# A two-layer attention encoder: second attention's outputs in 512-query groups, last norm on token rows, and query low halves one step behind

## The reference

```python
# layer 0: differential attention, 8 heads, two components of 64
s = einsum('bqhcd,bkhcd->bhcqk', q, k) * scale + rel_bias     # then masked softmax p
a = p[:, :, 0] - lam * p[:, :, 1]
o = rms_norm(einsum('bhqk,bkhe->bqhe', a, v), subln_w) * (1 - lam_init)
# layer 1: latent attention, 16 heads, 64 + 32 (rotary) query and key columns, 64 value columns
p = softmax(masked((q_nope @ k_nope + q_rope @ k_rope) * scale))
o = einsum('bhqk,bkhe->bqhe', p, v)
# each layer then: o @ w_o, norm, square(relu(u @ w1)) @ w2, norm
```

## Time and profile before

| | |
|---|---|
| Median of 3 runs (least, most) | 2934.26 us (2934.16, 2934.52) |
| Profiled execution | 2934.04 us |
| Its span, instructions | 2932.4 us, 37871 |
| Busy: TensorE, VectorE, ScalarE, GpSimd | 91%, 56%, 40%, 11% |
| First attention, a head of 427.50 to 490.40 | 62.90 us |
| Second attention, two heads from 1705.27 | 31.63 and 31.83 us |

### The profile page before, as it was taken

The page is one execution under the profiler, slowest core; times in us unless marked ns, Lnnn a source line. Parts: engine busy times, 40 slices in busy tenths (PEclk is TensorE's granted clock), DMA queues, the critical chain, the costliest instruction groups (busy, mean ns, idle before and its releaser), DMA issues.

```text
span 2932.4 us, 37871 instructions
## 1 busy us (share of the span) xinstructions
PE 2668.8 (91%) x12716; PEld 2189.5 (75%) x12716; DVE 1654.3 (56%) x2830; ACT 1163.9 (40%) x2093; POOL 328.5 (11%) x346
## 2 busy tenths in 40 slices
PE   3899989879999999999997888888699999999996
PEld 2677777767788888887776777777577888888884
DVE  4477777747653443543757777777376233232356
ACT  2365666634512213123454665566245122130323
POOL 0000000001110000160324222222010000000000
PEclk8999999989999999999999999999899999999997
DMA  8233333363342331412331111111633111111122
GB/s 316 74 90 103 111 93 104 92 224 90 101 136 85 90 118 50 137 57 68 117 95 23 28 29 30 29 27 43 220 90 87 57 50 50 43 50 50 50 80 79
DMA packets 333440, 254.17 MB, mean 87 GB/s; under 512 B 41192, under 2 KB 303639, under 8 KB 332319
## 3 DMA queue, kind: packets, MB, share of 16 engines
q1 hardware_dynamic: 317518, 194.21, 22.9%
q0 software_dynamic: 14736, 50.34, 5.6%
q10 hardware_dynamic: 1088, 8.39, 0.7%
HBM read 215.12 MB, written 33.59 MB: 85 GB/s over the span
## 4 chain that ended last, share of the span: by engine, by line
PE 63%; DVE 13%; ACT 11%; issue 9%; DMA 3%; DVEq 0%; ACTq 0%; SPq 0%; POOL 0%
PE PA L1693 31%; PE SC L1693 26%; DVE H L1219 2%; DVE soft L1608 2%; ACT H L749 2%; DVE W L1128 1%; ACT X L1054 1%; ACT X L765 1%; PE TB L1700 1%; DMA x_rows<-in_x 1%; ACT W L702 1%; PE SC L1801 1%; PE VB L1785 1%; DVE X L1630 1%; DMA attention_out<-ostage 1%
## 5 line engine op out<-in xcount | busy, mean ns | idle before, releaser
L1693 PE MATMUL PA<-U,W 128*128 128x512 f32 x3840 | 950.3, 402 | 81.5 <-DVE W L1128 44.4
L1693 PEld LDWEIGHTS PA<-U,W 128*128 128x128 f32 x3840 | 726.0, 191 | 251.9 <-issue 57.2
L702 ACT ACTIVATE W<-raw 128x1024 fp32r<-128x1024 f32 (+2 forms) x262 | 260.1, 994 | 816.4 <-PE PA L1693 390.1
L1693 PE MATMUL SC<-U,W 128*128 128x512 f32 x2064 | 481.1, 391 | 4.0 <-DVE W L1128 3.7
L1693 PEld LDWEIGHTS SC<-U,W 128*128 128x128 f32 x2064 | 387.2, 188 | 90.2 <-DVE W L1128 4.9
L1128 DVE TENSOR_TENSOR W<-raw,W 128x1024 fp32r<-128x1024 f32 (+2 forms) x262 | 315.4, 1204 | 99.6 <-ACT W L702 98.3
L1693 PE MATMUL PA<-H,W 128*128 128x512 f32 x1536 | 358.6, 392 | 3.2 <-DVE W L1128 3.2
L1693 PE MATMUL SC<-H,W 128*128 128x512 f32 x1536 | 354.4, 390 | 0.0
L1693 PEld LDWEIGHTS PA<-H,W 128*128 128x128 f32 x1536 | 288.5, 189 | 64.3 <-DVE W L1128 3.6
L1693 PEld LDWEIGHTS SC<-H,W 128*128 128x128 f32 x1536 | 288.4, 188 | 60.7 <-issue 1.0
L1392 DVE SCALAR_TENSOR_TENSOR X<-PA,aff,X 128x512 f32 (+1 forms) x80 | 60.0, 750 | 211.5 <-PE PA L1693 211.5
(11 more groups left out here) (221 smaller groups left out, 3037.3 us busy)
## 6 DMA issues: line engine op xcount, KB each, us to landing
raw<-in_ffn_w SPq DMA_DIRECT2D x160, 512.0 KB, 4.0
ada<-in_ada_w POOLq DMA_DIRECT2D x80, 512.0 KB, 4.6
U<-attention_out SPq DMA_DIRECT2D x4, 3584.0 KB, 17.5
raw<-in_da_w_qkv SPq DMA_DIRECT2D x24, 512.0 KB, 5.2
ada_first<-in_ada_w ACTq DMA_DIRECT2D x4, 2048.0 KB, 18.1
H<-H SPq DMA_DIRECT2D x32, 256.0 KB, 5.3
attention_out<-ostage SPq DMA_DIRECT2D x32, 256.0 KB, 2.9
raw<-in_da_w_o SPq DMA_DIRECT2D x16, 512.0 KB, 4.0
```

The lines of the kernel that those rows point to most:

```text
L702: nc.scalar.activation(W[:, slot, 0, 0:kt * P], raw[:, slot, 0:kt * P], ACT.Copy).then_inc(w_hi, 1)
L1693: ins = mm(bank, W[:, slot, a, kt * P:(kt + 1) * P], moving(b, kt)[:, cols], start=kt == first and (a, b) == SPLIT[0], stop=kt == last and ...
```

## The change

Three parts, with the counters that they need.

Second attention. Outputs come in two groups of four steps, 512 queries each, computed in step 4 (first group) and step 0 of the next head (second). The inverse row sums are spread by four 128x128 transposes into a transposition bank (`inverses1`), copied by ScalarE (`copy_l`), and VectorE scales both halves of the result at once (`scale_out`); ScalarE brings the scaled lower half up a step later, GpSimd adds (`out_sum1`) and takes the low half (`out_lo1`). GpSimd also takes over both `split_lo` of a head's weight slabs; ScalarE rounds the query slab two steps before the head that uses it. The transposed weights and values get other places in SBUF. One store per group, 64 rows by 512.

Last norm, second half. As tiles come out of the last product, they are transposed between products to token rows (`row_turn`, `row_copy`) and summed (`row_sum1`). What is left behind the last product: mean, one squared pass for each of four row blocks on ScalarE with its sum, and two passes for each on VectorE (`row_center`, `row_scale`), then a store of 512 KB for each.

First attention. `lo_piece0` of query piece 5 moves from the end of step 0 to step 1, that of piece 2 from the end of step 4 to step 5, the query slab's split from step 1 to step 2, and `MACS` is spread otherwise.

```diff
-MACS = {2: (0, 1), 3: (2,), 5: (3, 4), 6: (5,), 7: (6, 7)}
+MACS = {2: (0,), 3: (1,), 4: (2, 3), 6: (4, 5), 7: (6, 7)}
+I_LATE, V_GROUP, I_EARLY = 1, 2, 8
+def turn_of(s, part):
+    return part + (0 if s == 0 else s + 2 if s < 5 else 2 * s - 1)
+def evacuated(h, ix):
+    return 13 * h + ix + 1 - (ix > I_LATE) - (ix > I_EARLY)
...
# SyncE
+                    if l == 1 and hf == 1:
+                        sp.wait_ge(d_ready, E_MLP1 + E_LAST)
+                        for dst, src in ((rows_g, ln_g), (rows_b, ln_b)):
+                            sp.dma_start(dst, src[1, 1:2, :].to_broadcast([P, D])).then_inc(row_in, 16)
...
+                if not is_first(h):
+                    store_o1(h - 1, 1)
                 if final:
                     sp.wait_ge(HS[1]["pj_ready"], 4 * HEADS1)
-                    sp.wait_ge(HS[1]["o_stored"], 16 * 4 * (HEADS1 - 2))
                     load_o(1, 0, KT - 1)
-                for pair in range(4):
-                    store_o(1, h, pair, VD)
+                store_o1(h, 0)
...
# GpSimd, second attention
+            def out_sum1(h, g):
+                pool.wait_ge(HS[1]["o_sq"], 2 * h + g + 1)
+                nc.gpsimd.tensor_tensor(osum, omul[0:VD, :], obot, ALU.add).then_inc(HS[1]["o_sum"], 1)
+            def out_lo1(h, g):
+                pool.wait_ge(HS[1]["o_hi"], 2 * h + g + 1)
+                nc.gpsimd.tensor_tensor(ostage1[:, 1, :].bitcast(F32R), osum, ostage1[:, 0, :], ALU.subtract)\
+                    .then_inc(HS[1]["o_lo"], 1)
+            def split_lo1(g0, hi, kt):
+                slot = g0 % 2
+                pool.wait_ge(w_hi, g0 + 2 * hi + 1)
+                nc.gpsimd.tensor_tensor(W[:, slot, 1, 0:kt * P], raw[:, slot, 0:kt * P],
+                                        W[:, slot, 0, 0:kt * P].bitcast(F32), ALU.subtract).then_inc(w_lo, 1)
...
+            def heads1(h0, i, last=False):
...
+                if proj:
+                    split_lo1(g0 + 1, 2 * i, KVT)
+                if not is_first(h):
+                    out_sum1(h - 1, 1)
+                if proj:
+                    rope_q(1 - p, h + 1, 0)
+                if not is_first(h):
+                    out_lo1(h - 1, 1)
+                out_sum1(h, 0)
+                if proj:
+                    rope_q(1 - p, h + 1, 1)
+                    own.end_body()
+                out_lo1(h, 0)
+                if not last:
+                    split_lo1(g0 + 2, 2 * i, QT)
...
# ScalarE, first attention
-                    if proj and s == 1:
+                    if proj and s == 2:
                         split_hi(g0 + 1, 3 * i, KT, a0["pj_ready"], 6 * h + 5)
...
# ScalarE, second attention
+            def copy_l(h, g, bank):
+                act.wait_ge(a1["o_inv"], 2 * h + g + 1)
...
+                nc.scalar.activation(linv, bank[:, :], ACT.Copy).then_inc(a1["r_ready"], 1)
+            def out_bottom1(h, g):
+                act.wait_ge(a1["o_fin"], 2 * h + g + 1)
+                nc.scalar.activation(obot, omul[VD:P, :], ACT.Copy).then_inc(a1["o_sq"], 1)
+            def out_hi1(h, g):
+                act.wait_ge(a1["o_sum"], 2 * h + g + 1)
+                if not (is_first(h) and g == 0):
+                    act.wait_ge(a1["o_stored"], 16 * (2 * h + g))
+                nc.scalar.activation(ostage1[:, 0, :].bitcast(F32R), osum, ACT.Copy).then_inc(a1["o_hi"], 1)
...
                     if s == 1 and not is_first(h):
-                        out_bottom(h - 1, 3)
-                        out_hi(a1, h - 1, 3, VD, osum[0:VD, :])
-                    if s in (3, 5, 7):
-                        out_bottom(h, (s - 3) // 2)
-                        out_hi(a1, h, (s - 3) // 2, VD, osum[0:VD, :])
+                        out_bottom1(h - 1, 1)
+                    if s == 2 and not is_first(h):
+                        out_hi1(h - 1, 1)
+                    if s == 5:
+                        out_bottom1(h, 0)
+                    if s == 6:
+                        out_hi1(h, 0)
...
+                    if s == 0 and not is_first(h):
+                        copy_l(h - 1, 1, t1_bank(I_LATE, p))
+                    if s == 4:
+                        copy_l(h, 0, t1_bank(I_EARLY, p))
...
# ScalarE, the end
+            for q in range(4):
+                nc.scalar.activation(ada[:, q % 2, :, :].rearrange("p b n -> p (b n)"), rows_y[:, q, :], ACT.Square,
+                                     bias=row_mean[:, q:q + 1], accum_out=row_sq[:, q:q + 1]).then_inc(row_q, 1)
...
# VectorE, first attention
+                    if s == 1 and not is_first(h):
+                        lo_piece0(p, h, LAST_PIECE)
+                    if s == 5 and proj:
+                        lo_piece0(1 - p, h + 1, PIECE_DONE[4])
+                    if proj and s == 2:
                         split_lo(g0 + 1, 3 * i, KT)
...
-                    if s == 0 and not is_first(h):
-                        lo_piece0(p, h, LAST_PIECE)
-                    if proj and s in PIECE_DONE and PIECES[PIECE_DONE[s]][0] != "v":
+                    if proj and s in PIECE_DONE and PIECES[PIECE_DONE[s]][0] == "k":
                         lo_piece0(1 - p, h + 1, PIECE_DONE[s])
...
# VectorE, second attention
+            def scale_out(h, g):
+                dve.wait_ge(a1["o_ready"], 2 * h + g + 1)
+                dve.wait_ge(a1["r_ready"], 2 * h + g + 1)
+                if not (is_first(h) and g == 0):
+                    dve.wait_ge(a1["o_sum"], 2 * h + g)
+                nc.vector.tensor_tensor(omul, VB[:, :], linv, ALU.mult).then_inc(a1["o_fin"], 1)
...
# VectorE, the end
+            row_center(0)
+            for q in range(1, 4):
+                row_center(q)
+                row_scale(q - 1)
+            row_scale(3)
...
# TensorE, second attention
+            def inverses1(h, g, free, bank):
+                pe.wait_ge(a1["l_inv"], 2 * h + g + 1)
+                pe.wait_ge(a1["t_evac"], free)
+                for k in range(4):
+                    ins = nc.tensor.transpose(bank[:, k * P:(k + 1) * P], row_inv(4 * g + k).to_broadcast([P, P]), ident)
+                ins.then_inc(a1["o_inv"], 1)
+            def values1(h, g):
+                last = 4 * g + 3
+                pe.wait_ge(a1["o_fin"], 2 * h + g)
                 for j in range(last + 1):
+                    if j % 4 == 0:
+                        pe.wait_ge(a1["t_evac"], evacuated(h, turn_of(last, j // 4)))
+                    c0 = max(0, j - 4 * g) * P
                     for b in (1, 0):
+                        ins = mm(VB[:, c0:HALF], V1[:, j, :], AT1[g, b, j // 4][:, j % 4, c0:HALF],
+                                 start=j == 0 and b == 1, stop=j == last and b == 0)
...
# TensorE, the last products
+            def row_turn(t):
+                pe.wait_ge(d_evac, E_MLP1 + MLP_PRODUCTS - KT + t + 1)
+                if t >= 2:
+                    pe.wait_ge(row_y, t - 1)
+                for q in range(4):
+                    ins = transpose_to(row_bank(t)[:, q * P:(q + 1) * P], X[:, t, HALF + q * P:HALF + (q + 1) * P])
+                ins.then_inc(row_t, 1)
```

More of the change, by code:

```diff
@@ L677, in _ @@
             own.enter()
[L678 to L679 removed]
+            own.body(0, 2 * NH)
+            for n in range(NH):
+                rope_q(0, 0, n)
             own.end_body()
[L681 to L687 removed]
```

273 lines of the change are left out of this document (161 added, 112 removed).

## The result

The changed kernel takes 2912.77 us in the median of 4 runs (2911.42 to 2917.47), the kernel before 2934.39 beside it: ratio 0.9929, 95% interval 0.9912 to 0.9946. It is 21.6 us faster; the forecast was 45. The direction held and the size is less than half. The range (2868 to 2914) held by 1.2 us, and not for its reasons: it was drawn around cases 2 and 3, and neither came about as described. The profiled execution took 2912.53 us for a span of 2910.9.

What follows compares the result with a forecast made beforehand. TensorE, busy 91%, sets the first attention's pace; in the second it waits for VectorE and ScalarE; nothing hides the last norm. 2932.4 - 17 - 36 - 10 + 16 = 2885.4, plus 1.8: 2887, rounded up to 2889 us; range 2868 to 2914.

Steps and rivals of the forecast that it cites:

- cases 2 and 3: First attention rivals: 2, second slip not given back, 2905 us, chance 0.16; 3, swap hidden, 2873 us, chance 0.16.
- Part 1: Kernel's end: last norm's second half on token rows shortens the tail, -17 us (bounds -12 and -20).
- Part 2: Second attention: head from 31.7 to 29.3 us, -36 us over 15 heads; its last head, a further -10 us.
- the walk: Second attention: following VectorE's order through a head to get TensorE's waits; 2.4 and 1.0 us go, 1.6 come.
- The two on transposed low halves: Second attention: two TensorE waits like the 0.46 us on a transposed block's low half go, 1.0 us together.
- a step behind what they wait for: Second attention: ScalarE's new output copies stand later; it had idled 3.90 us before one copy, two to three before others.
- +52.5 against +62.7: -10 us: Second attention's last head: from its start to the product, without ScalarE's 11.28 us stand for a store (bounds -3, -14).
- the same 17.5 us from there to the product: Second attention's end: time from the last low half, at +34.5, to the product, taken as unchanged.
- Part 3: First attention: low halves, slab split and multiply-adds change places; +2.2 to +2.4 us for heads 1 to 7, +16 us.
- the swap's two DMAs landed 5.3 us after issue: First attention, queries' second half: swap lands at 454.8, TensorE waits 2.75 us, net +2.4 us.
- case 3: First attention rival: swap is hidden, landing in half the time when queues are idle; 2873 us, chance 0.16.
- The second slip: First attention, queries' first half: projection reusing the bank slips 2.35 us, given back by vanished waits; step's end moves -0.2 us.

Runs made afterwards that it cites:

- e3: Part 1 alone (last norm's second half on token rows) on the kernel before: 2916.21 us, ratio 0.9940.
- e10: Only the low halves of the second attention's two weight slabs moved to GpSimd, on the kernel before: 2921.08 us, ratio 0.9948.
- e11: On e1, ScalarE's rounding of the output put right behind its copy of the bottom rows, not one step later: 2896.20 us, ratio 0.9866.
- r1: The kernel before, unchanged, profiled again: single time 2934.88 us.
- e1: The changed kernel with Part 3 (first attention) undone: 2898.94 us, ratio 0.9879 to the kernel before.
- e7: On e1, the low halves of the second attention's weight slabs put back from GpSimd to VectorE: 2905.77 us, ratio 0.9904.
- e8: On e1, 12 of a head's 24 value products in the second attention left out: 2864.70 us, ratio 0.9770.
- e12: On e1, VectorE takes the low halves of the projected queries ahead of the next maximum, not behind it: 2923.98 us, ratio 0.9950.
- e9: On e1, the output projection's third weight slab and the residual's first half loaded before the second attention's last store: 2891.06 us, ratio 0.9847.
- e6: On e1, only Part 3's move of the first query half's low halves and the multiply-adds' new places: 2905.38 us, ratio 0.9909.
- e5: On e1, only Part 3's moves of the second query half's low halves and the second slab's split: 2912.23 us, ratio 0.9931.

## Why the prediction was wrong in size

**Part 1 was right**, term by term. -18.2 for -17: the transposes 0.5 cheaper, the tail 0.9 us shorter (in e3 5.0 us for 5.5 up to the mean, 9.7 for 9.6 in the passes, 3.2 for 3.6 behind them).

**Part 2, "29.3 us: 2.4 us a head, over 15 heads -36 us", is the step that failed**, in two terms.

First, the walk. The undisturbed step fell from 31.63 to 29.85, 1.78 us, some 26 over fifteen. The forecast had TensorE's listed waits shrink by 1.8 us (2.4 and 1.0 gone, 1.6 new). They shrank by 1.0: they sum to 4.7 us in an undisturbed head before and to 3.8 after. The two on transposed low halves went, but one of 0.80 us came at another place, and the wait before the query pieces is 1.57, not 1.35. TensorE's work fell by 0.7, where the forecast had 0.6. GpSimd was as forecast (14.8 us a head for 15.2; TensorE has no wait on its slab half). e10 shows what the slab halves are worth by themselves: 1.0 us of a head, more than half of the 1.78. There the wait of 2.35 us for the slab's low half becomes one of 0.91 for the query's, about the trade that the forecast had in it; the rest of part 2 brought 0.8. Part of what e10 gains is that VectorE works beside a busy GpSimd: the 128x256 form, 1170 ns in the earlier trace rows, takes 1.22 us in fifteen heads with GpSimd at work beside it, as the forecast said, and 0.43 in the one without. And e11 shows that the copies "a step behind what they wait for" brought nothing.

Second, the clock, which the forecast left out altogether. It worked from one undisturbed head. Of the some 26 us, 9.7 were lost to drops: 457.8 us measured against 15 x 29.87 = 448.1. Before, drops were as many, but a step with one took 31.63 to 31.84 against 31.63. TensorE's order in r1 shows why. The last waits of a head, without a drop, are the two of 1.0 us together that the forecast removed:

```profile
1806.61 0.66 PE L1700 MATMUL TB<-cst,X 128*128 128x128 f32 x4 [0.46 <-DVE H L1219]
1807.81 0.44 PE L1700 MATMUL PA<-cst,X 128*128 128x128 f32 x2 [0.54 <-DVE H L1219]
```

and in the step ahead, whose drop begins 23.4 us into it, the same two have no wait:

```profile
1775.75 0.60 PE L1700 MATMUL PA<-cst,X 128*128 128x128 f32 x4
1776.18 0.43 PE L1700 MATMUL TB<-cst,X 128*128 128x128 f32 x2
```

In both executions of the kernel before, every drop in these steps begins 22.9 to 24.8 us into its head, just ahead of these two waits, and they are what swallows it. After, drops begin some 7 us into the head, or 22 to 24 us; behind them stand waits that stay as long as they were (1.57) or the 0.26 us for the inverses' bank. There one costs 1.1 to 1.6 us and two cost 2.5 to 2.9. Other kernels:

| Kernel | step without | with one drop | with two |
|---|---|---|---|
| before (both executions, from the second step) | 31.63 | 31.63 to 31.84 | |
| after (both executions), e1 | 29.85 | 30.97 to 31.41 | 32.37 to 32.71 |
| e7 | 31.08 | 31.13 to 32.48 | 32.49 |
| e8 | 28.17 | 29.21 to 29.71 | |
| e12 | 32.28 | 32.71 to 32.80; its first two steps 33.96 and 33.89 | |

That a drop lengthens TensorE's instructions is shown by the rows, and so is that the waits close behind it shrink. A head's sum of waits does not sort the table (e12 has the most, and e7, with as much as the kernel before, pays from 0.05 to 1.4 us): it is the waits close behind the drop that count. In e7 the cheap drops begin 6.8 and 7.5 us into the head, ahead of two waits of 0.8 us together, the dear one at 23.5 with 0.3 us behind it. No run here could set the clock itself, so that this place decides the cost stays a reading of the traces.

**The last head, "+52.5 against +62.7: -10 us", gave 4.1.** The stand behind the store went as forecast. What the forecast had wrong is what holds the end then: it let the load and the store end the head, with the last low half at +34.5, 10.7 us sooner than before. It came 6.2 us sooner, measured from the last maximum, and stands behind no store but behind the last outputs: value products, scaling, copy, sum, rounding (2069.24 to 2079.40). The value products ran within a drop (eight in 3.76 us; 2.10 for the same eight at full clock, in the row of 1766.25), which is 1.7 us of the 4.4 missing; the others were not taken apart. The last tile's reload then landed later (6.9 us from issue at 2082.37 to the product at 2089.25, 5.3 before). Behind it stood a wait of 8 us that the forecast had counted as given, "the same 17.5 us from there to the product"; e9 shows that queue order made it and takes 5.3 us out.

**Part 3 came out at its size by chance.** The waits named on record add 0.85 us to an undisturbed head, not 2.4. The step that failed: "the swap's two DMAs landed 5.3 us after issue", carried to a new place in the queue. In the kernel before, a slab of 512 KB is issued 0.5 us ahead of the swap; here in r1:

```profile
442.40 0.40 SPq L310 DMA_DIRECT2D raw<-in_da_w_qkv  x1
442.90 1.33 SPq L368 DMA_DIRECT2D H<-H  x2
```

In the changed kernel 8.6 us lie between them (452.85 and 461.45 above), and the swap lands in 3.7 us in the median. e6 has both cases in one trace, the second half's swap at its old place (issued at 450.82, 0.5 us behind a slab) and the first half's at its new one (489.64, 6.8 us behind):

```profile
H<-H SPq DMA_DIRECT2D x2, 256.0 KB, 5.7
H<-H SPq DMA_DIRECT2D x2, 256.0 KB, 3.5
```

e5 has it the other way round. So case 3 of the rivals had the mechanism (a swap lands sooner when nothing is queued just ahead), but neither its size, half the time, nor its end, a hidden swap: TensorE waits 1.15 instead of 2.75 (1.22 in e5). By the Trainium skill (DMA: Bandwidth & Descriptors, section Anatomy of one DMA) 256 KB would take 2.6 us, an estimate, and the wait would vanish; but the page fits its rule to DMAs that GpSimd issues, and these are SyncE's. The measurement, 3.7, decides. The second slip was given back as forecast: 62.81 for 62.95 in e6. Two things made +17.9 of it. The waits give 5.1 us in six steps, and 2.6 more in the last one, where TensorE stands 5.37 us for the swap and two older waits give 2.8 back:

```profile
593.80 2.79 PE L1942 MATMUL SC<-H 128*128 128x512 f32 x8 [5.37 <-DMA H<-H]
```

The drops give the rest: some six in six steps after, one before (five more, 8.4 us), and some 3 us in the last step, with some seven for four. The stage began 1.2 us earlier. All four kernels with a piece of part 3 have more drops there than those without (three to eight in six steps, against one or two).

What stays open is why the clock falls more often in these orders. In undisturbed steps TensorE is busy 85% in the kernel before, 88% in e10 and 87% after, with nine, no and nine drops in fourteen steps (each kernel's second execution), so its busy share does not sort them. By the Trainium skill (TensorE: Matmul & The Clock Gate, section A second HAM failure mode: psum-queue depth-cycling) another kernel, which cycles through PSUM banks, idles for moments between groups of matmuls often enough that its clock swings between the two levels. The swings are seen here (1.00 and 0.53 in the rows of 1791 and 1793.5); which idle times cause them, no run tells.

## What to carry to other kernels

Read several turns of a loop, with the granted clock beside each, and forecast the undisturbed and the disturbed one apart: a wait close behind a drop of the clock swallows it, and who removes that wait pays for the drop. A DMA's landing time belongs to its place in the queue; when it moves, ask what is issued just ahead of it there. A step that is out of line may hold a stand ahead of the drop: look before you put it down to the clock. And undo a change part by part: the piece that looked smallest (two slab halves on GpSimd) is alone worth 15 us, where all of part 2 is worth 17, and part 3 left out gives 14 more.

## What the runs showed of the hardware

In the heads shown, a drop of TensorE's granted clock to 1.2 GHz lasts about 3.4 us and takes 1.7 us of full speed from it. Drops repeat in number: twice none in fourteen heads of one kernel, twice one in the same step of another. In the second attention one costs a step 0 to 1.6 us (1.7 in e12's first two), by the waits behind it; in the first attention 0.6 to 2.0, with the stand of the fourth step taken out.

The swap's two DMAs of 256 KB, issued by SyncE, land in 3.7 us in the median in the changed kernel, and in 5.3 in the kernel before, where a load of 512 KB was issued 0.5 to 1.4 us ahead of thirteen of the sixteen swaps.

VectorE slows beside GpSimd: a slab difference of 128x256 takes 1.22 us with GpSimd at work during 94% of it and 0.43 without, one of 128x512 1.77 us and 0.67.

On GpSimd an addition of 64x512 takes 1.29 us, and the difference for a 128x512 slab 1.28:

```profile
L716 POOL TENSOR_TENSOR tmp<-acc,tmp 64x512 f32<-64x512 f32 x2 | 2.6, 1289 | 3.9 <-ACT tmp L1161 3.9
L728 POOL TENSOR_TENSOR W<-raw,W 128x512 fp32r<-128x512 f32 x1 | 1.3, 1279 | 0.2 <-POOL tmp L721 0.2
```

The rotations' 32x512 takes 1.26 to 1.28 us in the changed kernel: the number of partitions makes no difference there, as the forecast assumed.
